# A two-block transformer kernel on one core: the compression weights' load moved to ACT's queue, the compression matmuls turned round, and the spatial bias added on TensorE

## The reference, cut to what matters

```python
def compress(kv, pe, w1, w2):          # kv (B,S,G,Dh): once for keys, once for values
    ch = kv.reshape(b, s // 16, 16, g, d)
    nc = 15                            # blocks of 32 positions at stride 16
    blocks = concatenate([ch[:, r:nc + r] for r in range(2)], axis=2) + pe
    hid = silu(einsum('bnlgd,lde->bnge', blocks, w1))       # w1: 32 x 64 x 64
    return einsum('bnge,ef->bngf', hid, w2)                 # w2: 64 x 64

def spatial_gating(uv, ln_g, ln_b, w_s, b_s):
    u, v = split(gelu(uv)); v = layer_norm(v, ln_g, ln_b)
    sv = einsum('gts,bcsgd->bctgd', w_s * tril, v) + b_s.T[None, None, :, :, None]
    return u * sv                      # 8 groups, chunks of 128 positions
```

## Time and profile before

| | |
|---|---|
| Median of 3 runs | 2663.34 us (2662.17 to 2671.37) |
| Profiled execution | 2671.37 us, its span 2669.6 us |
| PE, PEld busy | 2230.4 us (84%), 1633.3 us (61%) |
| DVE, ACT, POOL busy | 1528.6, 694.6, 772.3 us |
| DMA | 754.61 MB, mean 283 GB/s |

### The profile page before, as it was taken

One profiled execution on the slowest core, in us unless ns is written; L12 is line 12 of the kernel. 1 busy time (PEld: TensorE's weight loads), 2 busy tenths in 40 slices (PEclk: granted clock), 3 DMA queues, 4 the chain that ended last, 5 costly groups with the idle time before them and its releaser, 6 DMA issues.

```text
span 2669.6 us, 33108 instructions
## 1 busy us (share of the span) xinstructions
PE 2230.4 (84%) x12212; PEld 1633.3 (61%) x12212; DVE 1528.6 (57%) x2181; ACT 694.6 (26%) x1151; POOL 772.3 (29%) x658
## 2 busy tenths in 40 slices
PE   7999999999999999899567668777687766877668
PEld 7999999999999999899522223222232322322223
DVE  4455555455646686656665555665556555566552
ACT  5344554444434435444100000000000000000001
POOL 3000000000002433120354444544445444444441
PEclk9999999999999999999788999998999889989899
DMA  9534444455675444565699999999999999999996
GB/s 260 184 127 142 141 143 140 157 163 169 213 228 177 142 158 158 154 193 158 234 394 396 400 423 393 400 402 390 416 401 400 389 386 423 402 387 403 388 423 248
DMA packets 280704, 754.61 MB, mean 283 GB/s; under 512 B 11968, under 2 KB 213152, under 8 KB 213792
## 3 DMA queue, kind: packets, MB, share of 16 engines
q0 software_dynamic: 74432, 539.07, 49.7%
q1 hardware_dynamic: 205936, 214.23, 25.3%
q10 hardware_dynamic: 240, 0.07, 0.0%
HBM read 751.22 MB, written 2.10 MB: 282 GB/s over the span
## 4 chain that ended last, share of the span: by engine, by line
PE 59%; DMA 25%; issue 7%; DVE 7%; POOL 1%; ACT 1%; DVEq 0%; POOLq 0%; ACTq 0%; SPq 0%
PE PS L1552 39%; DMA EX<-in_peer_v,idx 22%; PE PS L1870 14%; DVE EX L1493 2%; DMA RAW<-in_peer_u,idx 2%; PE PS L1687 1%; DVE WL L993 1%; POOL EX L595 1%; PE PS L1607 1%; PE PS L1665 1%; DVE XL L1003 0%; PE PS L1675 0%; PE PS L1787 0%; POOL RAW L595 0%; PE PS L1689 0%
## 5 line engine op out<-in xcount | busy, mean ns | idle before, releaser
L1870 PE MATMUL PS<-EX,RK 128*128 128x512 f32 x2048 | 959.5, 620 | 396.5 <-ACT RK L972 207.8
L1870 PEld LDWEIGHTS PS<-EX,RK 128*128 128x128 f32 x2048 | 390.9, 197 | 964.5 <-issue 902.2
L1552 PE MATMUL PS<-XH,WH 128*128 128x256 f32 x3024 | 839.1, 286 | 11.7 <-DVE WL L993 8.0
L1493 DVE CUSTOM_DVE_ANT_0 EX<-RAW,RZ 128x2048 f32<-128x2048 f32 x256 | 582.4, 2291 | 449.7 <-DMA RAW<-in_peer_u,idx 422.1
L1552 PE MATMUL PS<-XH,WL 128*128 128x256 f32 x3024 | 832.7, 284 | 0.0
L1552 PE MATMUL PS<-XL,WH 128*128 128x256 f32 x3024 | 761.9, 284 | 5.0 <-DVE XL L1003 3.1
L993 DVE TENSOR_TENSOR WL<-RAW,WH 128x1024 fp32r<-128x1024 f32 x380 | 479.7, 1274 | 413.5 <-ACT WH L643 410.9
L1552 PEld LDWEIGHTS PS<-XH,WH 128*128 128x128 f32 x3024 | 582.0, 192 | 15.7 <-issue 9.7
L1552 PEld LDWEIGHTS PS<-XH,WL 128*128 128x128 f32 x3024 | 582.2, 193 | 0.0
L643 ACT ACTIVATE WH<-RAW 128x1024 fp32r<-128x1024 f32 x380 | 400.2, 1059 | 566.1 <-PE PS L1552 564.5
L1552 PEld LDWEIGHTS PS<-XL,WH 128*128 128x128 f32 x3024 | 539.9, 193 | 5.9 <-DVE XL L1003 3.5
(11 more groups left out here) (316 smaller groups left out, 1139.1 us busy)
## 6 DMA issues: line engine op xcount, KB each, us to landing
RAW<-in_w_in SPq DMA_DIRECT2D x110, 1024.0 KB, 5.1
RAW<-in_w_out SPq DMA_DIRECT2D x32, 1024.0 KB, 5.4
RAW<-in_w_ple_gate SPq DMA_DIRECT2D x16, 1024.0 KB, 5.4
RAW<-in_peer_wq SPq DMA_DIRECT2D x16, 1024.0 KB, 5.4
RAW<-in_w_up_a SPq DMA_DIRECT2D x8, 1024.0 KB, 5.4
RAW<-in_w_up_b SPq DMA_DIRECT2D x8, 1024.0 KB, 5.3
RAW<-in_peer_u,idx POOLq DMA_INDIRECT x256, 13.1
EX<-in_peer_v,idx POOLq DMA_INDIRECT x256, 12.5
```

Source lines behind the costliest of these rows:

```text
L1493: v.tensor_tensor_reduce(out=junk[k % 2], in0=ubuf[s], in1=znat[:, hf, :], scale=1.0, scalar=0.0, op0=ALU.mult, op1=ALU.add, accum_out=act ...
L1552: ins = mm(o[:, t, :], w[:, q, k, c], x[:, n, :], start=(begins and k == t == m == 0), stop=(ends and k == QUARTER_KT - 1 and m == len(pai ...
L1870: ins = mm(bank(4 * hf + c), diag[:, s, :], vbuf[s][:, 512 * c:512 * (c + 1)], start=False, stop=True, skip_group_check=True)
```

## The change

It has three parts.

1. The eight loads of `w1bd` and `w2bd` leave POOL's queue. POOL zeroes `w1bd` as before and raises a new semaphore; ACT issues the loads, behind its evacuation of the panel `q` 3 and ahead of the rounding of the panel `kv` 0 (`split_next("gl", 0)`).
2. In the compression the operands change places: `w1bd` (128 x 128) is stationary, 30 columns of `kab` move (15 blocks for each group pair). The result lies with the channels on the partitions, so the transposes (L1614) and the copy (L1059) go, and the product with `w2` stands behind `kv` 4 in place of `kv` 5.
3. The bias is loaded on one partition, and 16 matmuls of a row of ones with it add it in PSUM. DVE's additions (L1178) go; its multiplication reads PSUM itself.

```diff
@@ SP
-                    sp.dma_start(sgub.rearrange("p g n -> p (g n)"), T["sgu_b"][0].rearrange("g t -> (g t)").partition_broadcast(P)).then_inc(S["sgu_in"], 16)
+                    sp.dma_start(sgub, T["sgu_b"][0].rearrange("g t -> (g t)").unsqueeze(0)).then_inc(S["sgu_in"], 16)
@@ POOL
-            line.do(g.memset(w1bd, 0.0))
-            for s, kind in enumerate("kv"):
-                for hf in range(2):
-                    rows = slice(HD * hf, HD * (hf + 1))
-                    g.dma_start(w1bd[rows, s, :, rows], T[f"cmp_w1_{kind}"][0].rearrange("l d e -> d l e")).then_inc(S["cmp_in"], 16)
-                    g.dma_start(w2bd[rows, s, rows], T[f"cmp_w2_{kind}"][0]).then_inc(S["cmp_in"], 16)
+            g.memset(w1bd, 0.0).then_inc(S["w1_zeroed"], 1)
@@ ACT, behind the evacuation of q 3
+            a.wait_ge(S["w1_zeroed"], 1)
+            a.wait_ge(S["zero_ready"], 6)
+            for s, kind in enumerate("kv"):
+                for hf in range(2):
+                    rows = slice(HD * hf, HD * (hf + 1))
+                    a.dma_start(w1bd[rows, s, :, rows], T[f"cmp_w1_{kind}"][0].rearrange("l d e -> d l e")).then_inc(S["cmp_in"], 16)
+                    a.dma_start(w2bd[rows, s, rows], T[f"cmp_w2_{kind}"][0]).then_inc(S["cmp_in"], 16)
+
             split_next("gl", 0)
@@ DVE, behind kv 4 (hid and the wait for hid_turned); what follows stood behind kv 5
-                    v.wait_ge(S["hid_turned"], 1)
-                    turned = bank(6)[:, 0:2 * (SPANS + 1)].rearrange(...)[:, :, :, 0:NC_BLOCKS]
-                    v.tensor_copy(hid[:].rearrange("p s (t n) -> p s t n", t=2), turned).then_inc(S["hid_ready"], 1)
-                if j == 5:
                     v.wait_ge(S["kc_done"], 1)
@@ DVE, spatial gating
-                        do(v.tensor_tensor(gin[:]..., bank(4 + n)..., sgub[:, 2 * n:2 * n + 2, :]..., ALU.add))
-                        v.scalar_tensor_tensor(uT[:, 2 * n:2 * n + 2, :], gin[:].rearrange("p (t n) -> p t n", t=2), 0.25,
-                                               uT[:, 2 * n:2 * n + 2, :], op0=ALU.mult, op1=ALU.mult).then_inc(S["ob_ready"], 1)
-                        v.wait_ge(S["ob_ready"], n + 1)
+                        v.scalar_tensor_tensor(uT[:, 2 * n:2 * n + 2, :], tiles2(4 + n), 0.25, uT[:, 2 * n:2 * n + 2, :],
+                                               op0=ALU.mult, op1=ALU.mult).then_inc(S["ob_ready"], 1)
@@ PE, compression
-                            ins = mm(bank(2 + s)[0:SPANS, 0:P], blocks, w1bd[:, s, l, :], start=(l == 0), stop=(l == CMP_LEN - 1))
+                            ins = mm(bank(2 + s)[:, 0:2 * NC_BLOCKS], w1bd[:, s, l, :], rhs, start=(l == 0), stop=(l == CMP_LEN - 1))
@@ PE, behind kv 4
-                    for s in range(2):
-                        at = s * (SPANS + 1)
-                        ins = tr(bank(6)[:, at:at + SPANS], hidn[:, s, :], ident[0:SPANS, 0:SPANS])
-                    ins.then_inc(S["hid_turned"], 1)
-                if j == 5:
-
-                    pe.wait_ge(S["hid_ready"], 3)
@@ PE, spatial gating
-                                ins = mm(o, vn[:, c, g, :], sguT[:, g, :], start=True, stop=True)
+                                mm(o, vn[:, c, g, :], sguT[:, g, :], start=True, stop=False)
+                                ins = mm(o, ones[0:1, :], sgub[0:1, g * P:(g + 1) * P], start=False, stop=True)
```

More of the change, by code:

```diff
@@ L28 @@
 CMP_LEN, CMP_STRIDE = 32, 16
-SPANS = 2 * TOK // CMP_STRIDE - 1
 NC_BLOCKS = TOK // CMP_STRIDE - CMP_LEN // CMP_STRIDE + 1
@@ L120 @@
     "out_done",
-    "ident_ready", "ones_ready", "dist_ready", "half_ready", "zero_ready", "pad_zeroed", "wt_ready",
+    "ident_ready", "ones_ready", "dist_ready", "half_ready", "zero_ready", "w1_zeroed", "pad_zeroed", "wt_ready",
     "vec_t", "vecs_ready", "xss_ready", "xrt_ready", "xn_ready", "xt_done",
@@ L124 @@
     "kv_evac", "gl_ready", "gl_t", "gates_ready", "vt_done", "vall_ready", "dup_done", "kpad_a", "kpad_v",
-    "kab_ready", "hid_done", "hid_tanh", "hid_turned", "hid_ready", "kc_done", "kc_ready", "kcdup_done", "kcpad_ready",
+    "kab_ready", "hid_done", "hid_tanh", "hid_ready", "kc_done", "kc_ready", "kcdup_done", "kcpad_ready",
     "mean_done", "xc_ready", "vsq_ready", "var_done", "vrt_ready", "y_ready", "yt_done", "vn_ready", "sv_done",
@@ L197, in build @@
         pts = view(RG, 2880, 1024)
-        sgub = view(RG, 1280, BT, P)
+        sgub = RG[0:1, 1280:1280 + BT * P]
         sgun = view(RG, 2304, BT, P)
@@ L266, in build @@
         hid = sb("hid", [P, 2, 2 * NC_BLOCKS])
+        hidt = sb("hidt", [P, 2, 2 * NC_BLOCKS])
         kcT = sb("kcT", [P, 2, NCP])
@@ L271, in build @@
         th = sb("th", [P, 2, PANEL * 2])
-        hidt, hidn = (th[0:SPANS, n, 0:2 * P].rearrange("p (s e) -> p s e", s=2) for n in range(2))
         gin = sb("gin", [P, PANEL * 2])
@@ L711, in _ @@
                         a.wait_ge(S["hid_done"], s + 1)
-                        a.activation(hidt[:, s, :], bank(2 + s)[0:SPANS, 0:P], ACT.Tanh, scale=0.5).then_inc(S["hid_tanh"], 1)
+                        a.activation(hidt[:, s, :], bank(2 + s)[:, 0:2 * NC_BLOCKS], ACT.Tanh, scale=0.5).then_inc(S["hid_tanh"], 1)
             for j in range(2):
@@ L1053, in _ @@
                         v.wait_ge(S["hid_tanh"], s + 1)
-                        v.scalar_tensor_tensor(hidn[:, s, :], hidt[:, s, :], 1.0, bank(2 + s)[0:SPANS, 0:P], op0=ALU.add, op1=ALU.mult)\
+                        v.scalar_tensor_tensor(hid[:, s, :], hidt[:, s, :], 1.0, bank(2 + s)[:, 0:2 * NC_BLOCKS], op0=ALU.add, op1=ALU.mult)\
                             .then_inc(S["hid_ready"], 1)
                 if j == 4:
-                    v.wait_ge(S["hid_turned"], 1)
-                    turned = bank(6)[:, 0:2 * (SPANS + 1)].rearrange("p (s t n) -> p s t n", s=2, t=2)[:, :, :, 0:NC_BLOCKS]
-                    v.tensor_copy(hid[:].rearrange("p s (t n) -> p s t n", t=2), turned).then_inc(S["hid_ready"], 1)
-                if j == 5:
                     v.wait_ge(S["kc_done"], 1)
@@ L1605, in _ @@
                             part, at = l // CMP_STRIDE, l % CMP_STRIDE
-                            blocks = kab[:, 2 * s + part].rearrange("p t (n l) -> p (t n) l", l=CMP_STRIDE)[:, part:part + SPANS, at]
-                            ins = mm(bank(2 + s)[0:SPANS, 0:P], blocks, w1bd[:, s, l, :], start=(l == 0), stop=(l == CMP_LEN - 1))
+                            rhs = kab[:, 2 * s + part].rearrange("p t (n l) -> p t n l", l=CMP_STRIDE)[:, :, part:part + NC_BLOCKS, at]
+                            ins = mm(bank(2 + s)[:, 0:2 * NC_BLOCKS], w1bd[:, s, l, :], rhs, start=(l == 0), stop=(l == CMP_LEN - 1))
                         ins.then_inc(S["hid_done"], 1)
```

4 lines of the change are left out of this document (removed).

## The result

The changed kernel is slower: 2704.58 us (median of 4 runs, 2700.43 to 2706.43) against 2663.57 us, a ratio of 1.015, 95% interval 1.0135 to 1.0165, so +41.0 us. The forecast was 2677, and its range ended at 2684. The profiled execution has a span of 2709.9 us against 2669.6.

The account below looks back on a forecast made before the run. PE was taken to bound the kernel, busy nearly without a break where the change acts. The terms 9.5 + 2.0 - 1.1 + 3.5 = +13.9 us on the median 2663.3 gave 2677.2 us, range 2662 to 2684.

Parts of the forecast that it names:

- Part 1, the stand: Between q 3 and kv 0: issues hold ACT 11.5 us, less 1.95 slack, so PE stands 9.5 us.
- The queue's depth: ACT's queue at the eight loads: about 2500 runs outstanding, read from SP's long issues; ACT free when 5950 are gone.
- Part 1, the clock behind the stand: After PE's stand at kv 0: some 4.1 us at half speed, losing 2.0 us.
- Part 2, "0.0 us": Compression: weight load sets the pace, a pass stays at 0.110 us as in L1647, so 0.0 us.
- Part 2, the order: Around kv 5 and the main loop's start: transposes go, the w2 product moves one panel forward, -1.1 us.
- The new wait for `kcpad`: Behind kv 5: PE's first half of L1637 done at about 160.6, kcpad ready only at 161.2.
- Part 3, "+3.5 us": Gating bias: 16 more matmuls are 32 more passes, all on PE, +3.5 us.
- A single row saves nothing: Bias matmuls in the gating: 128 stationary and 128 moving columns, so one row costs a full pass; +3.5 us.
- My upper bound of 7.0: Gating bias: 7.0 us if a one-row pass breaks the pipeline and costs double.
- The cheap compression: Compression passes go by columns, -10.8 us: +3.1 us (2666.4) with the stand, -6.6 (2656.7) without; chance 0.08.
- the issues don't hold ACT: Between q 3 and kv 0: ACT's queue takes the loads freely; +4.2 us in all, 2667.5; chance 0.25.
- A reading: Slices of the profile page: PE busy to nine tenths or more from the second slice to the nineteenth.

Follow-up runs that it names:

- part 1 alone: Only the eight loads of w1bd and w2bd moved to ACT's queue, against the kernel before the change: 2676.59 us against 2663.2, ratio 1.0051.
- 60-column kernel: Kernel before with only the compression's operands turned, each matmul streaming its 30 columns twice: 2660.16 us, ratio 0.9983; again 2659.3, ratio 0.9992.
- part 2 alone: Only the compression's operands turned, loads on POOL's queue and bias on DVE, against the kernel before: 2674.56 us, ratio 1.0041.

## Why the prediction was wrong, point by point

- **Part 1, the stand: right, with some luck.** Forecast 9.5 us, measured 10.9 in the change and 12.0 alone. ACT's rounding was forecast at 80.7 and came at 81.64. But the issues held ACT for 13.8 us (67.69 to 81.53), not 11.5. That they began 1.5 us ahead of the 69.14 from which I counted hid most of this. The queue's depth was read too large from SP: 2500 runs outstanding, where the end of the last issue found about 1300 packets. A packet took 24.7 ns in this stretch (80.9% of 16 engines over 13.84 us for 7261 packets) in place of 20.3.
- **Part 1, the clock behind the stand: right.** Forecast 4.1 us at half speed and 2.0 us lost. In the changed kernel it was 3.0 us; 12.2 later at the compression, less the stand of 10.9, gives 1.3. In part 1 alone it was 5.2 us, and 1.8 lost.
- **Part 2, "0.0 us": the step that failed.** I set the length of a pass by L1647 and it was right, 0.110 us, as the first passes after the change and the 60-column kernel show. What I took for granted is that the clock would stay at 1.00. L1647's eight passes last 1 us, and the clock fell only 2.8 us after the compression's start. I gave the clock a term behind the stand, where PE is idle, and none where PE is busy with little. Its size: +10.4 us in the compression, and in `kv` 4 behind it what the next point gives.
- **Part 2, the order: right.** Forecast -1.1. The 60-column kernel goes from 133.70 to 163.54 in place of 133.91 to 165.06, 29.8 against 31.2, so -1.3. The new wait for `kcpad`, 0.5 us, was forecast at 0.6. In the changed kernel +1.2 stands in the ledger, so 2.5 us went to the clock.
- **Part 3, "+3.5 us": failed twice.** With 128 rows it measured +3.5. With one row it is 16.6, and 1.9 behind it. "A single row saves nothing" was right for the load and wrong for its overlap: alternating with 128 rows doubled the pass, and again the clock fell. My upper bound of 7.0 doubled only the 32 added passes. All 64 took 0.21, which is 13.3 us and so 9.8 more than before even at a clock of 1.00, and the bound left the clock out. Of the 15.0 us over the forecast that makes 6.3 for the lost overlap and 8.7 for the clock, an estimate from these rates.
- **Sum.** Forecast 9.5 + 2.0 - 1.1 + 3.5 = 13.9. Measured by the ledger 12.2 + 10.4 + 1.2 + 16.6 + 1.9 - 1.7 = 40.6. Of the difference of 26.7, 10.4 + 2.5 is the clock in and behind the compression and 15.0 the one-row matmuls.
- **The rivals.** None of them was it. The cheap compression (passes by columns) was refuted by the changed kernel's first 26 passes, 0.109 us each with 30 columns at a clock of 1.00. That the issues don't hold ACT was refuted by the timeline.
- **The -1.7 in the later stages** is no gain of the change. PE's waits there are the same in both traces once the stretches are laid over each other: 6.9 us in 740 to 1000 before and in 782.3 to 1042.3 after; 9.0 us in 1000 to 1320 and in 1042.3 to 1362.3. What differs is the clock behind one of these waits, 2.24 or 2.25 us for `XL`, which ends at 926.17 before and at 968.41 after. Before and after:

```profile
928.00:930.00 2.00, 2.00 (x11) 2.00 (x11) 2.00 (x4) 0.55 (x1) 0.22 (x3) 0.50 0.00 0
970.00:972.00 2.00, 2.00 (x19) 2.00 (x19) 2.00 (x4) 0.79 (x1) 0.46 (x5) 1.00 0.00 0
```

Before, the clock is 0.50 for 3.3 us, which costs 1.6. At this wait it falls in seven of the fourteen traces of this case and stays in the other seven, among them variants without any edit near it: which of the two comes is chance of the execution, as far as the runs show.
- **A reading.** The earlier trace rows show an 8 in the seventeenth slice, so PE isn't busy to nine tenths in all of the second to the nineteenth; the change acts in the second to the tenth, and nothing hung on it.

## What to carry to other kernels

A rate read from a short stretch holds only for the clock of that stretch: when an edit makes PE's matmuls narrow for many passes in a row, in columns or in rows, look for a longer stretch of such work and at its granted clock, and price the panel behind it too. Where the weight load sets the pace, further moving columns are free up to the load's length (30 and 60 columns 64 bytes apart, and 120 in runs of 15, all took 0.11 us a pass), and here they were worth 10 us in the compression because they kept the clock. A DMA of many short runs belongs on a queue whose engine has slack for it, and several of them belong in several places.

## What the runs showed of the hardware that was not expected

- The granted clock fell while PE was busy without a gap: with 30 moving columns for each fp32 load of 128 columns (part 2 alone: the first such pass at 119.4, the fall at about 122.8 us), and not with 60 columns or 120. With one-row matmuls it fell, with 128-row matmuls of the same number it did not.
- fp32 passes of 128 rows and of one row in turns of two took 0.21 us each at 2.4 GHz; in turns of eight 0.136; with a single turn 0.11.
- 120 moving fp32 columns 64 bytes apart took 0.20 us a pass, in runs of 15 side by side 0.112; 60 columns 64 bytes apart still hid behind the load at 0.111.
- On ACT's queue a DMA of 2048 runs of 256 bytes was issued in 0.63 to 0.73 us, and the DMA of 64 runs behind it was held 1.3 to 5.0 us. When it was released, 1030 to 1890 packets of the queue were still outstanding.
- At one and the same wait of PE, 2.24 or 2.25 us for `XL`, the granted clock fell to 0.50 for some 3 us in seven of fourteen traces and stayed at 1.00 in seven.
